# First norm of a decoder layer: modulation sums in chunks of 2, 2, 4, 4, 2, 2 tiles, with four column tiles of TensorE

## The reference

```python
c_act = jax.nn.silu(c)
mod = c_act @ w_ada[l] + b_ada[l]
sh1, sc1, g1, sh2, sc2, g2 = [m[:, None, :] for m in jnp.split(mod, N_MOD, axis=-1)]
h = rms_norm(x, norm1_w[l]) * (1.0 + sc1) + sh1
proj = h @ w_in[l]
```

## Time and profile before

| | |
|---|---|
| median of 3 runs (lowest, highest) | 1298.03 us (1297.01, 1298.38) |
| the profiled execution | 1298.59 us |
| its span, first to last instruction | 1296.8 us |
| TensorE busy | 1257.6 us, 97% |
| VectorE busy | 998.0 us, 77% |
| ScalarE busy | 612.3 us, 47% |
| mean granted TensorE clock | 0.983 |

### The profile page before, as it was taken

The page is one execution under the profiler, slowest core; times in us unless marked ns, Lnnn a source line. Parts: engine busy times, 40 slices in busy tenths (PEclk is TensorE's granted clock), DMA queues, the critical chain, the costliest instruction groups (busy, mean ns, idle before and its releaser), DMA issues.

```text
span 1296.8 us, 20722 instructions
## 1 busy us (share of the span) xinstructions
PE 1257.6 (97%) x7190; PEld 1109.5 (86%) x7190; DVE 998.0 (77%) x1298; ACT 612.3 (47%) x851; POOL 50.3 (4%) x98
## 2 busy tenths in 40 slices
PE   5899899999999999999999999999999999999997
PEld 5888899998988878888888888888888888888886
DVE  4787799999998989788888797879767766545454
ACT  3335555555556644455444444444444444434342
POOL 0000100031130000000000000000000000000000
PEclk9789899999999999999999999999999999999999
DMA  9999798888798899758777777776666676556553
GB/s 337 386 385 334 271 306 279 277 286 291 250 305 278 299 350 365 267 168 297 244 222 238 239 231 241 233 249 212 186 188 193 191 264 211 195 194 194 195 195 114
DMA packets 155988, 329.44 MB, mean 254 GB/s; under 512 B 11493, under 2 KB 20438, under 8 KB 155026
## 3 DMA queue, kind: packets, MB, share of 16 engines
q1 hardware_dynamic: 152352, 318.49, 74.1%
q0 software_dynamic: 3280, 9.66, 2.2%
q10 hardware_dynamic: 290, 0.44, 0.1%
HBM read 322.77 MB, written 4.19 MB: 252 GB/s over the span
## 4 chain that ended last, share of the span: by engine, by line
PE 86%; DVE 5%; DMA 4%; ACT 2%; issue 2%; SPq 0%; DVEq 0%; ACTq 0%
PE bank L1266 24%; PE bank L1274 13%; PE bank L1331 6%; PE bank L1329 6%; PE bank L1330 6%; PE bank L1012 5%; PE bank L1014 5%; PE bank L1013 5%; PE bank L999 3%; PE bank L1001 3%; PE bank L1002 3%; DMA pc<-in_w_ada 3%; DVE acc_c L1425 2%; DVE wlo L1413 1%; PE bank L959 1%
## 5 line engine op out<-in xcount | busy, mean ns | idle before, releaser
L678 ACT ACTIVATE whi<-wraw 128x1024 fp32r<-128x1024 f32 x408 | 425.1, 1059 | 580.5 <-PE bank L1274 227.4
L1413 DVE TENSOR_TENSOR wlo<-wraw,whi 128x1024 fp32r<-128x1024 f32 x404 | 490.9, 1221 | 238.5 <-ACT whi L678 237.1
L1266 PE MATMUL bank<-h,whi 128*128 128x512 f32 x1400 | 334.7, 391 | 0.9 <-DVE h L1675 0.8
L1266 PEld LDWEIGHTS bank<-h,whi 128*128 128x128 f32 x1400 | 257.1, 188 | 51.6 <-issue 1.2
L1274 PEld LDWEIGHTS bank<-h,wlo 128*128 128x128 f32 x1400 | 179.6, 191 | 6.9
L1274 PE MATMUL bank<-h,wlo 128*128 128x256 f32 x1400 | 181.7, 283 | 0.0
L999 PE MATMUL bank<-h,whi 128*128 128x256 f32 x512 | 148.8, 291 | 5.2 <-DVE h L1438 5.2
L1001 PE MATMUL bank<-h,whi 128*128 128x256 f32 x512 | 145.9, 285 | 0.0
L1002 PE MATMUL bank<-h,wlo 128*128 128x256 f32 x512 | 145.7, 285 | 0.0
L1329 PE MATMUL bank<-whi,act_hi 128*128 128x512 f32 x336 | 130.7, 389 | 0.0
L1330 PE MATMUL bank<-wlo,act_hi 128*128 128x512 f32 x336 | 130.7, 389 | 0.0
(11 more groups left out here) (244 smaller groups left out, 1328.6 us busy)
## 6 DMA issues: line engine op xcount, KB each, us to landing
wraw<-in_w_up SPq DMA_DIRECT2D x176, 512.0 KB, 3.8
araw<-in_w_ada SPq DMA_DIRECT2D x128, 512.0 KB, 5.6
wraw<-in_w_in SPq DMA_DIRECT2D x112, 512.0 KB, 5.1
wraw<-in_w_down SPq DMA_DIRECT2D x88, 512.0 KB, 4.1
pc<-in_w_ada SPq DMA_DIRECT2D x48, 512.0 KB, 11.5
wraw<-in_w_out SPq DMA_DIRECT2D x32, 512.0 KB, 6.5
pc<-in_w_ada SPq DMA_DIRECT2D x32, 256.0 KB, 7.0
x<-in_x SPq DMA_DIRECT2D x2, 1024.0 KB, 7.7
```

The lines of the kernel that those rows point to most:

```text
L678: act.activation(whi[:, slot], wraw[:, slot], ACT.Copy).then_inc(s_hi, 1)
L1266: pe.matmul(ps[bank0 + f], whi[:, (ph.unit0 + j) % RING, k, f * P:(f + 1) * P], h[:, kk].rearrange("p a t -> p (a t)"), start=(kk == 0), s ...
L1413: dve.tensor_tensor(wlo[:, slot], wraw[:, slot], whi[:, slot].bitcast(F32), ALU.subtract).then_inc(s_lo, 1)
```

## The change

The chunks become 2, 2, 4, 4, 2, 2 tiles. The unit groups follow: units 0 to 2, 3 to 5, 6 to 11, 12 to 17, 18 to 20, 21 to 23.

TensorE sums the first two tiles (`ROWT`) of every chunk in all 16 pieces. silu(c) is laid out as `csil32`, 32 columns per piece of which only the first is not zero. One float32 matmul per piece has these 32 columns as weights and the 512 shift and scale columns of two tiles as the moving operand; piece r goes to column tile r % 4 of the array, that is to PSUM partitions 32*(r % 4) and on. ScalarE copies the 128x512 bank into `rowsum`, and four matmuls with a column of ones turn it into columns. VectorE sums the other two tiles of the two 4-tile chunks only. A piece's buffer is free when TensorE and, in those chunks, VectorE have read it. The bank of the sums is the same for all chunks, so TensorE's first batch of a chunk waits for the scale and shift of the chunk before.

The places change too: all four unit loads of the start come behind chunk 0's 16 pieces; in a group of three units all four batches of four pieces and the sum stand behind its first unit; in a group of six the batches stand behind units 0, 1, 2 and 3 and the sum behind unit 3. ScalarE's copy of chunk n's rows stands behind `first_hi(U0[n]+1)`.

```diff
-CHUNK = (4, 4, 4, 2, 2)
+CHUNK = (2, 2, 4, 4, 2, 2)
+ROWT = 2
...
-PE_TILES = ((2, 5, 8, 11), (2, 5, 8, 11), (2, 7, 12), (3, 7, 11), (3, 7, 11))
-
-PE_AFTER = ((0, 1, 3, 4), (0, 1, 3), (0, 1, 3), (0, 1, 1))
-SUM_AFTER = (4, 4, 4, 1)
-
-LOADS_AT = ((3, 7, 11, 15, 15, 15), (3, 7, 11, 15, 15, 15), (3, 7, 11, 15, 15, 15), (5, 10, 15))
...
+ROWS_AFTER = {3: (0, 0, 0, 0), 6: (0, 1, 2, 3)}
+SUM_AFTER = {3: 0, 6: 3}
+
+LOADS_AT = {3: (5, 10, 15), 6: (3, 7, 11, 15, 15, 15)}
+LOWS_AT = {3: (5, 10, 15), 6: (2, 4, 8, 11, 15, 15)}
+PC_OF_DVE = [i for i in range(CHUNKS * KT) if CHUNK[i // KT] > ROWT]
...
+                    sp.wait_ge(s_pcp, i - PC_RING + 1)
+                    if i - PC_RING in PC_OF_DVE:
+                        sp.wait_ge(s_pcd, pieces_of_dve(i - PC_RING) + 1)
...
-                if r == 13:
-                    load_in(0)
-            for v in range(1, RING):
+            for v in range(RING):
                 load_in(v)
...
+            def chunk_rows(c):
+
+                act.wait_ge(s_pcp, (c + 1) * KT)
+                if c:
+                    act.wait_ge(s_red, c)
+                act.activation(rowsum[:].rearrange("p a t -> p (a t)"), ps[7][:, 0:2 * ROWT * P], ACT.Copy).then_inc(s_rows, 1)
+
             for k in range(KT // 2):
+                if k == 6:
+                    chunk_rows(0)
...
-                    if v == U0[n] + 1:
+                    if v == U0[n] + (n > 0):
+                        if n:
+                            chunk_rows(n)
                         chunk_hi(n)
...
+            def first_rows(c, batch):
+
+                if c and batch == 0:
+                    pe.wait_ge(s_redc, c)
+                for r in range(4 * batch, 4 * batch + 4):
+                    i, q = c * KT + r, r % 4 * 32
+                    pe.wait_ge(s_pc[i % PC_RING], (i // PC_RING + 1) * 16)
+                    pe.matmul(ps[7][q:q + 32, :], csil32[:, r, :], pc[:, i % PC_RING, :, 0:ROWT * P], start=(batch == 0),
+                              stop=(batch == 3), skip_group_check=True, tile_position=(0, q)).then_inc(s_pcp, 1)
 
             def chunk_columns(c):
 
...
+                n = CHUNK[c]
+                pe.wait_ge(s_rows, c + 1)
+                for part in range(2):
+                    for tile in range(ROWT):
+                        k = part * n + tile
+                        last = pe.matmul(ps[7][:, k:k + 1], rowsum[:, part, tile * P:(tile + 1) * P], ones[:, 0:1], start=True, stop=True)
+                if n > ROWT:
+                    pe.wait_ge(s_pcd, pieces_of_dve((c + 1) * KT))
+                    for part in range(2):
+                        for tile in range(ROWT, n):
+                            k = part * n + tile
+                            last = pe.matmul(ps[7][:, k:k + 1], acc_c[:, c % 2, part, (tile - ROWT) * P:(tile - ROWT + 1) * P], ones[:, 0:1],
+                                             start=True, stop=True)
                 last.then_inc(s_red, 1)
 
-            pe.wait_ge(s_csilu, 1)
-            first_piece(2)
+            pe.wait_ge(s_csil32, 2)
+            first_rows(0, 0)
+            first_rows(0, 1)
             for k in range(KT // 2):
...
+                if k == 5:
+                    first_rows(0, 2)
+                    first_rows(0, 3)
...
-                    for r, at_ in zip(PE_TILES[m + 1], PE_AFTER[m]):
+                    for batch, at_ in enumerate(ROWS_AFTER[units_in(m)]):
                         if u - U0[m] == at_:
-                            first_piece((m + 1) * KT + r)
-                    if u - U0[m] == SUM_AFTER[m]:
+                            first_rows(m + 1, batch)
+                    if u - U0[m] == SUM_AFTER[units_in(m)]:
                         chunk_columns(m + 1)
```

More of the change, by code:

```diff
@@ L68, with pieces_of_dve, units_in @@
 PC_RING = 12
-PE_TILES = ((2, 5, 8, 11), (2, 5, 8, 11), (2, 7, 12), (3, 7, 11), (3, 7, 11))
-PE_AFTER = ((0, 1, 3, 4), (0, 1, 3), (0, 1, 3), (0, 1, 1))
-SUM_AFTER = (4, 4, 4, 1)
-LOADS_AT = ((3, 7, 11, 15, 15, 15), (3, 7, 11, 15, 15, 15), (3, 7, 11, 15, 15, 15), (5, 10, 15))
-LOWS_AT = ((2, 4, 8, 11, 15, 15), (2, 4, 8, 11, 15, 15), (2, 4, 8, 11, 15, 15), (5, 10, 15))
-PC_OF_PE = [c * KT + r for c in range(CHUNKS) for r in PE_TILES[c]]
-PC_OF_DVE = [i for i in range(CHUNKS * KT) if i not in PC_OF_PE]
+ROWS_AFTER = {3: (0, 0, 0, 0), 6: (0, 1, 2, 3)}
[3 more added lines that the diff above has]
+PC_OF_DVE = [i for i in range(CHUNKS * KT) if CHUNK[i // KT] > ROWT]
+def pieces_of_dve(i):
+    return sum(e < i for e in PC_OF_DVE)
+def units_in(m):
+    return U0[m + 1] - U0[m]
 OUT0, UP0 = PROJ_UNITS, PROJ_UNITS + 32
@@ L239, in build @@
         diag0 = at(Z + 88 * K + 512, "diag0", [TB, P])
-        acc_c = at(Z + 94 * K, "acc_c", [2, 2, CT * P])
+        acc_c = at(Z + 94 * K, "acc_c", [2, 2, (CT - ROWT) * P])
+        csil32 = at(Z + 102 * K, "csil32", [KT, 32])
+        rowsum = at(Z + 76 * K, "rowsum", [2, ROWT * P])
         htmp0 = at(Z + 48 * K, "htmp0", [4, SEQ])
@@ L334, in build @@
         s_pcp = sem("s_pcp")
+        s_rows = sem("s_rows")
+        s_csil32 = sem("s_csil32")
         s_pcd = sem("s_pcd")
@@ L531, in _ @@
                     load_first((m + 1) * KT + r)
-                    for _ in range(LOADS_AT[m].count(r)):
+                    for _ in range(LOADS_AT[units_in(m)].count(r)):
                         load_in(v)
@@ L586, in _ @@
             st = Steps(gp, s_p)
+            gp.memset(csil32[:], 0.0).then_inc(s_csil32, 1)
             gp.memset(ones[:], 1.0).then_inc(s_cst, 1)
@@ L686, in _ @@
             act.activation(csilu, ps[0][:, 0:16], ACT.Silu).then_inc(s_csilu, 1)
+            act.wait_ge(s_csil32, 1)
+            act.activation(csil32[:, :, 0], ps[0][:, 0:16], ACT.Silu).then_inc(s_csil32, 1)
             act.wait_ge(s_cst, 5)
@@ L948, in _ @@
             pe.transpose(ps[1][:, 0:97], rows[0:97, 0, :], ident[0:97, 0:97]).then_inc(s_prmT, 1)
[L950 to L962, removed]
@@ L964, in chunk_columns @@
-            def chunk_columns(c):
[L966 to L970, removed]
+            def first_rows(c, batch):
[6 more added lines that the diff above has]
+                              stop=(batch == 3), skip_group_check=True, tile_position=(0, q)).then_inc(s_pcp, 1)
@@ L984, in _ @@
                 last.then_inc(s_xT, 1)
-            first_piece(5)
-            first_piece(8)
-            first_piece(11)
+                if k == 5:
+                    first_rows(0, 2)
+                    first_rows(0, 3)
             chunk_columns(0)
@@ L1417, in first_piece @@
                 dve.wait_ge(s_pc[i % PC_RING], (i // PC_RING + 1) * 16)
-                a, new = acc_c[:, c % 2, :, 0:CHUNK[c] * P], pc[:, i % PC_RING, :, 0:CHUNK[c] * P]
+                a, new = acc_c[:, c % 2], pc[:, i % PC_RING, :, ROWT * P:CHUNK[c] * P]
                 if r == 0:
@@ L1423, in first_piece @@
                 else:
-                    dve.wait_ge(s_pcd, PC_OF_DVE.index(i))
+                    dve.wait_ge(s_pcd, pieces_of_dve(i))
                     ins = dve.scalar_tensor_tensor(out=a, in0=new, scalar=csilu[:, r:r + 1], in1=a, op0=ALU.mult, op1=ALU.add)
@@ L1428, in chunk @@
             def chunk(c):
-                n, cols, sums = CHUNK[c], slice(CH0[c], CH0[c + 1]), ps[6 + c % 2]
+                n, cols, sums = CHUNK[c], slice(CH0[c], CH0[c + 1]), ps[7]
                 dve.wait_ge(s_red, c + 1)
@@ L1439, in chunk @@
                     e = k - CH0[c]
-                    if c + 1 < CHUNKS and e % 2:
+                    if c + 1 < CHUNKS and CHUNK[c + 1] > ROWT and e % 2:
                         first_piece((c + 1) * KT + e // 2)
@@ L1447, in _ @@
             dve.wait_ge(s_csilu, 1)
[L1448 to L1462, removed]
+            parameters()
+            dve.wait_ge(s_rt, 1)
+            st.then(dve.reciprocal(ss, rstd))
+            for b in range(TB):
+                dve.tensor_scalar(diag0[:, b], ident[:, ::-1] if b else ident[:], ss[:, b:b + 1], None, ALU.mult).then_inc(s_diag0, 1)
+            angles()
+            first_lo(0)
             dve.wait_ge(s_xTc, KT // 2)
             chunk(0)
+            first_lo(1)
             for c in range(CHUNKS - 1):
@@ L1467, in _ @@
                 for r in range(KT):
-                    if r not in PE_TILES[c + 1] and r >= CHUNK[c] // 2:
+                    if CHUNK[c + 1] > ROWT and r >= CHUNK[c] // 2:
                         first_piece((c + 1) * KT + r)
-                    for _ in range(LOWS_AT[c].count(r)):
+                    for _ in range(LOWS_AT[units_in(c)].count(r)):
                         if v < RING:
```

4 lines of the change are left out of this document (removed).

## The result

The changed kernel takes 1308.11 us (median of 4 runs, 1307.26 to 1309.48) where the kernel before takes 1298.20 beside it: a ratio of 1.0081, 95% interval 1.0068 to 1.0093. Forecast were 1309 us, within 1299 to 1330. The profiled execution took 1307.29 us, its span 1305.5, which is 8.7 longer than the span of before.

A forecast was written before the change was run, and what follows sets the result against it. It took the DMA as the bound in the first 160 us and TensorE after that. Unit 24 starting at 166.3 instead of 155.1 us, 11.2 later, gave 1298.03 + 11 = 1309 us, range 1299 to 1330.

The forecast's parts named there:

- the walk: Count of TensorE's units, batches and sums up to unit 24: it starts at 166.3 us against 155.1, 11.2 later.
- The price of a batch: Four new matmuls on TensorE: one pass of 0.43 us per piece, so 1.7 us a batch.
- a sign of being wrong: In the timeline, a batch in under 1 us or over 3 would show the prediction wrong.
- the likeliest case in my list: TensorE's batches in order, pass by pass: 0.43 us a piece, range 1304 to 1320; chance 0.50 including its clock variant.
- the rival "together": On TensorE the column tiles run together, a batch costs 0.87 us: 5 to 7 us later, 1303; chance 0.26.
- Its steps: Together case: chunk 3's sum 104, units 10 and 11 112, next sum 129, units 16 to 18 137.5, last sum 145.
- the mis-sized term: Together case, last four pieces asked for after unit 18: about 2 + 3 us, to 142.7, sum 145.
- The price of the stream: DMA loads of the smaller chunks: pieces of 0.75 us instead of 0.69 cost 1.9 us of the stream.
- SyncE's waits: Ahead of chunk 2's sum, load 4 and pieces 12 to 15 of chunk 1 wait: 2 us added.
- The clock: Rival on TensorE: units after the new matmuls run slow more often, +21 us, 1319; chance within the 0.50 of pass by pass.
- slow stretches: On TensorE, one of units 4 and 5 slow (5.3 us against 2.9), and 2.5 us at units 10 and 11.
- VectorE's relief: Less summing on VectorE is worth at most its own last wait, 3.90 us, already in the unit count.

The follow-up runs named there:

- e2: The changed kernel, but all 16 pieces of a chunk go to the same column tile: 1342.62 us, ratio 1.0344 to the kernel before.
- e7: The changed kernel with chunk 1's first batch moved ahead of unit 0: 1306.08 us, ratio 1.0056 to the kernel before.
- e4: The changed kernel with chunk 5's first batch behind unit 16 and its second behind unit 17, not both behind unit 18: 1304.41 us.
- e9: The changed kernel with the moves of e4, e6 and e7 together: 1302.52 us, ratio 1.0031 to the kernel before.
- e12: e9 with one unit more in front of chunk 2's and chunk 3's sums (behind units 4 and 10): 1299.56 us, ratio 1.0013 to the kernel before.
- e6: The changed kernel with ScalarE copying chunk n's rows ahead of the high part of unit U0[n]+1, not behind it: 1307.32 us.

## Why the prediction was right

**Direction and place: right.** In the changed kernel unit 24's shift (8.6 us) is the span's (8.7), and most of the loss sits where the walk put it, ahead of the sum of 8 tiles (7.3 us by the walk, 7.2 measured). The walk's milestone for 8 tiles was 77 and 76.89 was measured; for 12 tiles 106.1 and 105.62; for 14 tiles 134.6 and 130.69; for 16 tiles 152.0 and 149.63; unit 24 at 166.3 and 163.67. The profiled execution was put at 1309.5 and took 1307.29.

**The price of a batch: wrong.** I chose 1.7 us, on the argument that the second pass of a piece has to wait for its first and holds up the next tile. Measured are 0.96 per batch where two follow each other and about 1.2 with the unit behind it, so a batch in under 1 us, which I had named as a sign of being wrong, did appear. The Trainium skill (TensorE: Matmul & The Clock Gate, Part 3) says that matmuls on different column tiles run at the same time, and the trace agrees; by e2 the four tiles give 3.62/1.06, a factor of 3.4 (3.75/1.19, or 3.2, with the neighbouring unit's share). So the likeliest case in my list was not the one that came true: the mechanism was that of the rival "together", with its ring of 12 buffers.

**Why that rival's 1303 was too low.** Its steps were 104, 112, 129, 137.5 and 145; measured were 105.62, 112.59, 130.69, 139.06 (end of unit 18) and 149.63. Up to unit 18 it was 1.6 us short: 0.6 at unit 12 already, and 1.1 over the next four batches, the 0.3 per batch that the neighbouring unit pays. The rest is the mis-sized term: the last four pieces, for which I gave 2 + 3 us after unit 18; they were summed at 146.81 to 147.86, since in this list each of them is released by one matmul of the first batch and none can be asked for ahead. That my own number came out near is luck in part, because two errors offset each other: from the sum of 12 tiles to that of 14 the walk had 28.5 us and 25.1 were measured (four batches at 1.7 instead of 1.2, and a slow stretch priced 1.1 too high); from there to the last scale and shift it had 17.4 and 18.9 were measured, since the last pieces and their batches took 8.8 (139.06 to 147.86) instead of 6.9.

**The price of the stream: half right.** 1.9 us for 32 more half pieces was of the right size (1.5 in e7 for the stretch to 100 us). What the walk added by estimate, 2 us for SyncE's waits, was measured by e7 as 2.0. The last requests are another 3.4 (e4). Both together, with the copies first, moved unit 24 by 7.1 (e9), and with the 1.5 of the stream that is the whole 8.6. The places of the sums are not in that figure: one unit more ahead of them moved unit 24 by 0.5 (e12), though the median time fell by 3.0. How the loss divides is known to about 1 us only.

**The clock: right to leave it out as a case, wrong in the sum.** I charged slow stretches of 2.4 us for unit 4 and 2.5 for units 10 and 11. In this execution unit 4 ran at full clock (76.71 to 79.67), units 10 and 11 took 7.15 us, 1.4 over full; in e6, e7 and e9 unit 4 took 4.4 us, so that term comes and goes. The new matmuls, although only one weight column of 32 is not zero, went with a clock of 1.00 from 58 to 68.5 us, where TensorE did nothing else and waited between pieces; from 69 to 75 it was 0.72. The one-column matmuls of before had been followed by 0.50 from 68.7 to 75.

**VectorE's relief: right.** 38 us less work on it bought nothing; TensorE's wait of 3.90 us for it was replaced by its waits for the last four pieces.

## What to carry to other kernels

When a stream is the bound, a ring buffer that an in-order engine frees at written places of its list is only as long as the next such place allows: put the first read of a chunk before anything that waits, and count how many requests lie behind each place. Splitting transfers finer starts the first consumer earlier, but what counts is the work left undone when the last transfer lands; here 10 us won at the start were lost by the second chunk. And a wait seen on one engine should be followed to the others that wait for the same event (ScalarE's copy, VectorE's low part) before it is priced.

## What the hardware showed that I had not expected

- Float32 matmuls with 32-column weights and 512 moving columns on four column tiles run together although each is two passes: 1.92 us for eight, 3.62 us for four on a single tile.
- Behind such a batch the next 128-column matmul begins late: unit and batch take 4.06 us where the unit alone takes 2.87 and a batch behind another one 0.96, so by estimate 0.1 us is lost at each of the two changes. The Trainium skill (TensorEngine Tiling (Array Packing), Key Properties) says that a change of tiling mode drains TensorE, which would be such a loss; no run here took the change away alone.
- A matmul that arrives alone for its piece takes 1.05 us in the timeline (its two passes in turn), as much as a batch of four that lie ready (1.06), so a batch gains from the tiles only if its pieces have landed.
